# Projections and the last feed-forward piece by token half, and each feed-forward as one stage

## The chip, the cores and the metric

The kernel runs as one program on one core of a Trainium2 chip. The metric is the time of one execution in microseconds (us). The engines are TensorE (PE; its weight loads are shown as PEld), VectorE (DVE), ScalarE (ACT), GpSimd (POOL) and SyncE (SP), which here only issues DMAs. Each engine runs its own list of instructions in order, and semaphores order the engines among each other.

## The reference, cut to what matters

A residual `x` of 1024 tokens by 1024 features (and a context of 256 tokens) passes two mixing layers and then a second block. Every layer begins with a norm over the features of a token and ends with a projection whose result is added to `x`:

```python
x = x + gt * (y @ out_e)                    # even layer, with context; then norm_o, in_o
x = x + gt * (y @ out_o)                    # odd layer (RWKV scan and a convolution)
x = rmsnorm(x, final_g)
x = layernorm(ALPHA * x + 0.5 * swiglu(x, ffn1_w1, ffn1_w3, ffn1_w2), ln1_g, ln1_b)
m = mixer(x, w_in, ...) @ w_out             # sparse attention and a gated MLP
x = layernorm(ALPHA * x + m, ln2_g, ln2_b)
x = layernorm(ALPHA * x + 0.5 * swiglu(x, ffn2_w1, ffn2_w3, ffn2_w2), ln3_g, ln3_b)

def swiglu(x, w1, w3, w2): return (silu(x @ w1) * (x @ w3)) @ w2     # 1024 -> 2816 -> 1024
```

A norm needs sums over all 1024 features of a token, so it needs the whole result of the projection before it for that token, and nothing of other tokens.

## The kernel before, in words

**Layout.** `xT` stays on the chip: 128 partitions, `KD` = 8 feature tiles, 1280 columns of tokens (1024 and the context). Tokens are worked in chunks: `MAIN_CHUNKS` are two halves of 512, `ALL_CHUNKS` adds the 256 of the context.

**Products in two parts.** Each fp32 operand is cut in a high part (ScalarE, `high_part`) and the rest as low part (VectorE, `low_part`), both as fp32r. `Weights.product` issues for each of the k tiles of 128 features three matmuls: high by high, high by low, low by high (lines 318, 319, 320). An output tile of 128 features over 1024 tokens is 2 x 8 x 3 = 48 matmuls of 512 columns.

**The weight ring.** `Weights` has two slots of raw, high and low weights. `load` waits until the slot's raw weights have been cut and issues a DMA on SP's queue, `cut_high` waits for the DMA and for the tile that used the slot before, `cut_low` follows on VectorE. `in_turn` writes ScalarE's and VectorE's order: weights of tiles 0 and 1, then for each tile m first the cut for m + 2 and then the work that finishes tile m. The ring belongs to a stage (`nc.Block`): a stage's first load is issued when all engines have left the stage before.

**Heads.** A stage begins with a head that makes the parts of its right operand: `Cut` (and `LoadedCut`, from `y_out` in DRAM) or `Norm`. ScalarE and VectorE do the first two weight cuts and then the head. A `Norm` with `centre` subtracts the mean, squares on ScalarE into two buffers, and sums with matmuls by `avg` on the PE (line 420), for both halves; then for each chunk come the root, the reciprocal (line 465), the scaling (468) and the parts (450, 482). GpSimd adds the bias to `xT` later.

**Combine stages** (`out_e`, `out_o`, `out_2`). 8 tiles over all chunks. VectorE adds each tile to `xT` (`gated_update`, line 672; `deepnorm_update`, line 680). `Totals` adds up the tiles (squares of ScalarE where the next norm does not centre), and `Totals.reduce` makes the mean on the PE behind the last tile (lines 187, 191).

**Feed-forward** (`ffn_stage`). The hidden 22 tiles are worked in `PIECES` of 8, 8 and 6. Each piece is two stages: `up`, two tiles (w1, w3) for a hidden unit, gated and cut on ScalarE and VectorE, and `down`, `product_stage` with 8 output tiles. That is six stages, each with its own ring. `out_stage` does the last norm and stores the output.

Of the kernel before, what the change touches and what calls it, by code (L numbers as in the profile page):

```python
# [8 lines left out]
P = 128  # L9
# [73 lines left out]
def program(nc, A):  # L83
# [16 lines left out]
    with root:  # L100
# [55 lines left out]
        class Totals:  # L156


            def __init__(self, ctx, name, chunks, squares):
                self.chunks, self.squares = chunks, squares  # L160
                width = chunks[-1][0] + chunks[-1][1]
                space = sb(ctx, f"{name}_totals", [P, 3 if squares else 1, width])
                self.acc, self.sq, self.width = space[:, 0], space[:, 1:3] if squares else None, width

            def tile(self, n):
                return self.sq[:, n % 2] if self.squares else xT[:, n, 0:self.width]

            def square(self, act, n):

                if n >= 2:  # L170
                    act.wait_ge(summed.h, summed.base + n - 1)
                nc.scalar.activation(self.sq[:, n % 2], xT[:, n, 0:self.width], ACT.Square).then_inc(squared.h, 1)

            def add(self, dve, n):
                if self.squares:
                    dve.wait_ge(squared.h, squared.base + n + 1)
                if n == 0:
                    nc.vector.tensor_copy(self.acc, self.tile(0)).then_inc(summed.h, 1)
                else:
                    dve.wait_ge(summed.h, summed.base + n)  # L180
                    nc.vector.tensor_tensor(self.acc, self.acc, self.tile(n), ALU.add).then_inc(summed.h, 1)

            def reduce(self, pe):
                n = KD - 1
                pe.wait_ge(summed.h, summed.base + n)
                for c, (t, w) in enumerate(self.chunks):
                    nc.tensor.matmul(bank(STAT_BANKS[c], w), avg[:, :], self.acc[:, t:t + w], start=True, stop=False)
                if self.squares:
                    pe.wait_ge(squared.h, squared.base + KD)
                for c, (t, w) in enumerate(self.chunks):  # L190
                    nc.tensor.matmul(bank(STAT_BANKS[c], w), avg[:, :], self.tile(n)[:, t:t + w], start=False,
                                     stop=True).then_inc(totalled.h, 1)

            def end(self):
                summed.base += KD - 1
                totalled.base += len(self.chunks)
                if self.squares:
                    squared.base += KD

        with ExitStack() as ctx:  # L200
# [5 lines left out]
            totals = Totals(ctx, "x", ALL_CHUNKS, True)  # L206
# [2753 lines left out]
```

## Time and profile before

| | |
|---|---|
| time, median of 3 runs | 4350.43 us (4343.89 to 4352.59) |
| profiled execution | 4352.45 us, its span 4350.5 us |
| PE busy | 3604.8 us, 83% of the span |
| VectorE busy | 1917.5 us, 44% |
| ScalarE busy | 1092.0 us, 25% |
| GpSimd busy | 84.7 us, 2% |
| mean granted TensorE clock of the span | 0.924 |
| DMA | 280.08 MB, mean 64 GB/s |

The span runs from the first to the last instruction. A matmul's end is modelled, so that the busy times of matmuls that follow each other closely overlap; their cost is better read from the distance of their starts. The idle time in brackets is that of the engine just before the instruction, with what released it. A granted clock of 1.00 is TensorE's upper level (2.4 GHz), 0.50 its lower one (1.2 GHz).

### The profile page before, as it was taken

To read this page: it belongs to the slowest core of one execution; us is meant where nothing else is said; L and a number is where in the kernel's file an instruction comes from. 1 tells how busy PE (TensorE), PEld (TensorE's weight loads), DVE (VectorE), ACT (ScalarE), POOL (GpSimd) and SP (SyncE) were. 2 spreads that over 40 slices of the span, in tenths; PEclk is the share of its full clock that TensorE was granted. 3 is DMA by queue.
4 is the path that set the end of the run, shared out by engine and by line. 5 is a ranking of instruction groups with operands and counts; after the bars stand their busy time and mean duration, and the time that the engine had idled before them with its cause. 6 is when DMAs were issued, how large, how long until landed. Compare 5 with 4: busy or idle time off the path is not lost. (4 is left out here: it accounts for less than half of the span.)

```text
span 4350.5 us, 67259 instructions
## 1 busy us (share of the span) xinstructions
PE 3604.8 (83%) x30260; PEld 2892.8 (66%) x30260; DVE 1917.5 (44%) x2670; ACT 1092.0 (25%) x1640; POOL 84.7 (2%) x83
## 2 busy tenths in 40 slices
PE   1999879997667777548999989889778979899997
PEld 1887668874256676436877778657556758777775
DVE  6554355445465556464211212267783352121224
ACT  2110221023333343212111101145464131011112
POOL 0000000000000000000000000020000020000000
PEclk9999999998589999769999999989899989999998
DMA  4232201223722212321111011111000111111111
GB/s 162 90 116 91 103 31 62 84 83 132 251 61 66 71 48 61 137 98 39 49 39 46 33 58 39 43 42 35 6 1 1 39 42 36 41 57 44 44 44 53
DMA packets 141677, 280.08 MB, mean 64 GB/s; under 512 B 7976, under 2 KB 83112, under 8 KB 141136
## 3 DMA queue, kind: packets, MB, share of 16 engines
q1 hardware_dynamic: 120912, 223.14, 16.0%
q10 hardware_dynamic: 20480, 52.65, 3.2%
q8 instruction: 238, 3.90, 0.4%
q14 instruction: 47, 0.39, 0.0%
HBM read 224.09 MB, written 51.42 MB: 63 GB/s over the span
## 5 line engine op out<-in xcount | busy, mean ns | idle before, releaser
L318 PE MATMUL PS<-ffn_x_high,ffn_up_wh 128*128 128x512 f32 x1408 | 554.7, 394 | 59.2 <-DVE ffn_up_wl L286 29.9
L319 PE MATMUL PS<-ffn_x_low,ffn_up_wh 128*128 128x512 f32 x1408 | 553.1, 393 | 0.0
L320 PE MATMUL PS<-ffn_x_high,ffn_up_wl 128*128 128x512 f32 x1408 | 552.7, 393 | 0.0
L286 DVE TENSOR_TENSOR ffn_up_wl<-ffn_up_raw,ffn_up_wh 128x1024 fp32r<-128x1024 f32 x88 | 108.4, 1232 | 648.0 <-ACT ffn_up_wh L283 647.8
L318 PEld LDWEIGHTS PS<-ffn_x_high,ffn_up_wh 128*128 128x128 f32 x1408 | 267.9, 190 | 119.0 <-DVE ffn_up_wl L286 31.6
L318 PE MATMUL PS<-ffn_hid_high,ffn_down_wh 128*128 128x512 f32 x704 | 281.1, 399 | 59.5 <-DVE ffn_down_wl L286 59.5
L320 PEld LDWEIGHTS PS<-ffn_x_high,ffn_up_wl 128*128 128x128 f32 x1408 | 267.4, 190 | 56.5
L319 PEld LDWEIGHTS PS<-ffn_x_low,ffn_up_wh 128*128 128x128 f32 x1408 | 267.7, 190 | 55.8
L319 PE MATMUL PS<-ffn_hid_low,ffn_down_wh 128*128 128x512 f32 x704 | 279.5, 397 | 0.0
L320 PE MATMUL PS<-ffn_hid_high,ffn_down_wl 128*128 128x512 f32 x704 | 279.1, 396 | 0.0
L283 ACT ACTIVATE ffn_up_wh<-ffn_up_raw 128x1024 fp32r<-128x1024 f32 x88 | 93.2, 1060 | 734.2 <-PE PS L320 594.8
L318 PE MATMUL PS<-in_o_high,in_o_wh 128*128 128x512 f32 (+1 forms) x608 | 229.0, 377 | 21.2 <-DVE in_o_low L482 18.6
L318 PE MATMUL PS<-in_e_high,in_e_wh 128*128 128x512 f32 (+1 forms) x576 | 209.7, 364 | 24.5 <-DVE in_e_low L482 23.1
L319 PE MATMUL PS<-in_o_low,in_o_wh 128*128 128x512 f32 (+1 forms) x608 | 228.0, 375 | 0.0
L320 PE MATMUL PS<-in_o_high,in_o_wl 128*128 128x512 f32 (+1 forms) x608 | 227.7, 375 | 0.0
L319 PE MATMUL PS<-in_e_low,in_e_wh 128*128 128x512 f32 (+1 forms) x576 | 206.2, 358 | 0.0
L320 PE MATMUL PS<-in_e_high,in_e_wl 128*128 128x512 f32 (+1 forms) x576 | 205.7, 357 | 0.0
L286 DVE TENSOR_TENSOR ffn_down_wl<-ffn_down_raw,ffn_down_wh 128x1024 fp32r<-128x1024 f32 (+1 forms) x48 | 54.5, 1137 | 326.4 <-ACT ffn_down_wh L283 326.4
L318 PEld LDWEIGHTS PS<-ffn_hid_high,ffn_down_wh 128*128 128x128 f32 x704 | 135.9, 193 | 90.7 <-DVE ffn_down_wl L286 62.0
L320 PEld LDWEIGHTS PS<-ffn_hid_high,ffn_down_wl 128*128 128x128 f32 x704 | 135.5, 193 | 29.1
L319 PEld LDWEIGHTS PS<-ffn_hid_low,ffn_down_wh 128*128 128x128 f32 x704 | 135.9, 193 | 28.3
L318 PEld LDWEIGHTS PS<-in_o_high,in_o_wh 128*128 128x128 f32 x608 | 115.5, 190 | 43.6 <-issue 18.6
(418 smaller groups left out, 6544.8 us busy)
## 6 DMA issues: line engine op xcount, KB each, us to landing
ffn_up_raw<-in_ffn_up SPq DMA_DIRECT2D x88, 512.0 KB, 3.5
norm_e_t<-in_ada SPq DMA_DIRECT2D x32, 512.0 KB, 4.1
in_o_raw<-in_in_o SPq DMA_DIRECT2D x32, 512.0 KB, 3.6
ffn_down_raw<-in_ffn_down SPq DMA_DIRECT2D x32, 512.0 KB, 3.6
scan_tin<-scan_in SPq DMA_DIRECT2D x10, 1536.0 KB, 10.1
scan_in<-um ACTq DMA_DIRECT2D x20, 641.0 KB, 5.0
in_e_raw<-in_in_e SPq DMA_DIRECT2D x24, 512.0 KB, 3.6
scan_tin<-scan_in SPq DMA_DIRECT2D x10, 1024.0 KB, 13.2
```

What stands on the lines that cost most here:

```text
L283: return nc.scalar.activation(out, x, ACT.Copy)
L286: return nc.vector.tensor_tensor(out, x, high.bitcast(fp32), ALU.subtract)
L318: nc.tensor.matmul(out, wh, xh, start=k == 0, stop=False)
L319: nc.tensor.matmul(out, wh, xl, start=False, stop=False)
L320: last = nc.tensor.matmul(out, wl, xh, start=False, stop=k == kt - 1)
```

## The change

- `Totals` takes groups of chunks. The three combine stages run over items (group, tile): eight tiles for the first half of the tokens, then the same eight for the rest, so every weight tile is loaded and cut twice. Each group is reduced on its own, the first behind item 8.
- `Norm` gets `early` chunks. For these the centring (behind item 8), squares (9), variance sums (10), root and reciprocal (11) and for norms in place the scaling (12, 13) are done inside the stage before. The next stage's head does only the rest. What a head does ahead of the first weight cuts moves to `lead_act` and `lead_dve`: centring, squares and variance sums of the second half, or the roots.
- `ffn_stage` is one block with one ring for all 76 items: 16 up, 8 down, 16 up, 8 down, 12 up, and 16 down items by half. At each change from up to down, the products of two tile halves are issued for all hidden units but the last, and then those for the last. PSUM is used in four quarters. The last feed-forward also holds the last norm and the stores of the output; `out_stage` and `project_stage` are gone.

The core of the diff:

```diff
 class Norm(Cut):
+    def lead_act(self, act):
+        for c in self.late():
+            if self.centre:
+                self.squares(act, c)
+            else:
+                self.root(act, c)
+
+    def lead_dve(self, dve):
+        if self.centre:
+            for c in self.late():
+                self.centre_chunk(dve, c)
+        if not self.early:
+            self.invert(dve, 0)
+        if not self.early or not self.in_place:
+            self.scale(dve, 0, range(KD))
...
+    def early_pe(self, pe, i):
+        if self.centre and i == 10:
+            self.var_sums(pe, 0)
+
+    def early_act(self, act, i, total):
+        if self.centre:
+            if i == 9:
+                self.squares(act, 0)
+            if i == 11:
+                self.root(act, 0)
+        elif i == 9:
+            act.wait_ge(totalled.h, total + 1)
+            self.root(act, 0)
+
+    def early_dve(self, dve, i, total):
+        if self.centre and i == 8:
+            dve.wait_ge(totalled.h, total + 1)
+            self.centre_chunk(dve, 0)
+        if i == 11:
+            self.invert(dve, 0)
+        if self.in_place and i in (12, 13):
+            self.scale(dve, 0, range(4 * (i - 12), 4 * (i - 12) + 4))
...
+def combine_stage(name, w_dram, rhs, chunks, groups, update, squares, norm, cut=Cut):
+    items = [(gi, m) for gi in range(len(groups)) for m in range(KD)]
...
+            for i, (gi, m) in enumerate(items):
+                s = i % 2
+                pe.wait_ge(w_low[s].h, w_low[s].base + i // 2 + 1)
+                pe.wait_ge(evacuated[s].h, evacuated[s].base + i // 2)
+                for c in groups[gi]:
...
+                    last = ring.product(pe, PS[:, at:at + w], s, parts, 0, KD, t, w, ready if m == 0 else None)
+                last.then_inc(tile_done[s].h, 1)
+                if i == KD:
+                    reduce(0)
+                norm.early_pe(pe, i)
+            reduce(1)
...
-def ffn_stage(name, w_up, w_down, head_of):
+def ffn_stage(name, w_up, w_down, head, norm, is_last):
     PIECES = [(0, 8), (8, 8), (16, 6)]
+    tiles = []
+    for p, (first, n_hid) in enumerate(PIECES):
+        both = [("down", p, m, (0, 1)) for m in range(KD)]
+        if p == len(PIECES) - 1:
+            both = [("down", p, m, (c,)) for c in range(2) for m in range(KD)]
+        tiles += [("up", p, m, (0, 1)) for m in range(2 * n_hid)] + both
...
+                            if kind == "down" and m == 0 and chunks[0] == 0:
+                                first, n_hid = PIECES[p]
+                                pairs = (first + n_hid) // 2
+                                turns = [(g, 0), (g, 1)] if chunks == (0, 1) else [(g, 0), (g + 1, 0)]
+                                pe.wait_ge(stored[0].h, stored[0].base + pairs)
+                                pe.wait_ge(stored[1].h, stored[1].base + pairs - 1)
+                                for q, c in turns:
+                                    product(q, c, range(n_hid - 1))
+                                pe.wait_ge(stored[1].h, stored[1].base + pairs)
+                                for q, c in turns:
+                                    product(q, c, range(n_hid - 1, n_hid))
+                                g = turns[-1][0] + 1
+                                continue
+                            for c in chunks:
+                                product(g, c)
+                            if g == TAIL + KD:
+                                reduce(0)
+                            norm.early_pe(pe, g - TAIL)
...
-        with ExitStack() as odd:
-            combine_stage("out_o", A["out_o"], yT, MAIN_CHUNKS, gated_update(mods["o"][2], False), True)
+            with ExitStack() as odd:
+                combine_stage("out_o", A["out_o"], yT, MAIN_CHUNKS, BY_CHUNK, gated_update(mods["o"][2]), True, final_norm)
+            ffn_stage("ffn1", A["ffn1_up"], A["ffn1_down"], final_norm, ln1, False)
+                mixer_stage(mT, ln1)
+                combine_stage("out_2", A["w_out"], mT, MAIN_CHUNKS, BY_CHUNK, deepnorm_update, False, ln2)
+            ffn_stage("ffn2", A["ffn2_up"], A["ffn2_down"], ln2, ln3, True)
```

## Rows read from the trace of the kernel before

**Rows 1.** Groups by line: busy us, mean ns | idle before, releasers.
```profile
L318 PE MATMUL PS<-ffn_x_high,ffn_up_wh 128*128 128x512 f32 x1408 | 554.7, 394 | 59.2 <-DVE ffn_up_wl L286 29.9 <-DVE ffn_x_low L286 16.8 <-DVE ffn_x_low L482 12.5
...
L318 PE MATMUL PS<-ffn_hid_high,ffn_down_wh 128*128 128x512 f32 x704 | 281.1, 399 | 59.5 <-DVE ffn_down_wl L286 59.5
```

**Rows 2.** Timeline of PE, feed-forward 1: start, us, engine line op [idle before].
```profile
2223.29 0.79 PE L318 MATMUL PS<-ffn_hid_high,ffn_down_wh 128*128 128x512 f32 x1 [10.49 <-DVE ffn_down_wl L286]
...
2320.85 0.80 PE L318 MATMUL PS<-ffn_x_high,ffn_up_wh 128*128 128x512 f32 x1 [7.46 <-DVE ffn_up_wl L286]
...
2507.17 0.80 PE L318 MATMUL PS<-ffn_hid_high,ffn_down_wh 128*128 128x512 f32 x1 [10.15 <-DVE ffn_down_wl L286]
```

**Rows 3.** Timeline of ACT and DVE, one tile of the second combine stage.
```profile
1960.21 1.06 ACT L283 ACTIVATE out_o_wh<-out_o_raw 128x1024 fp32r<-128x1024 f32 x1 [6.27 <-PE PS L320]
...
1961.30 1.23 DVE L286 TENSOR_TENSOR out_o_wl<-out_o_raw,out_o_wh 128x1024 fp32r<-128x1024 f32 x1 [6.11 <-ACT out_o_wh L283]
...
1964.85 1.23 DVE L181 TENSOR_TENSOR out_o_totals<-out_o_totals 128x1024 f32<-128x1024 f32 x1 [1.13 <-ACT out_o_totals L172]
...
1971.09 1.06 ACT L283 ACTIVATE out_o_wh<-out_o_raw 128x1024 fp32r<-128x1024 f32 x1 [6.27 <-PE PS L320]
```

**Rows 4.** Timeline of DVE: the last update of four stages.
```profile
594.17 1.68 DVE L672 SCALAR_TENSOR_TENSOR xT<-PS,mod_eg,xT 128x1024 f32<-128x1024 f32 x2 [9.27 <-PE PS L320]
...
2014.55 1.28 DVE L672 SCALAR_TENSOR_TENSOR xT<-PS,mod_og,xT 128x1024 f32<-128x1024 f32 x1 [7.24 <-PE PS L320]
...
2814.18 1.22 DVE L680 SCALAR_TENSOR_TENSOR xT<-xT,PS 128x1024 f32<-128x1024 f32 x1 [5.68 <-PE PS L320]
...
3482.27 1.22 DVE L680 SCALAR_TENSOR_TENSOR xT<-xT,PS 128x1024 f32<-128x1024 f32 x1 [8.40 <-PE PS L320]
```

**Rows 5.** Timeline of PE: the first product of five stages.
```profile
96.04 0.77 PE L318 MATMUL PS<-in_e_high,in_e_wh 128*128 128x512 f32 x1 [21.86 <-DVE in_e_low L482]
...
617.37 0.76 PE L318 MATMUL PS<-in_o_high,in_o_wh 128*128 128x512 f32 x1 [17.76 <-DVE in_o_low L482]
...
2035.76 0.76 PE L318 MATMUL PS<-ffn_x_high,ffn_up_wh 128*128 128x512 f32 x1 [16.79 <-DVE ffn_x_low L286]
...
2857.59 0.76 PE L318 MATMUL PS<-in_high,in_wh 128*128 128x512 f32 x1 [9.41 <-DVE in_low L482]
...
3523.05 0.77 PE L318 MATMUL PS<-ffn_x_high,ffn_up_wh 128*128 128x512 f32 x1 [9.41 <-DVE ffn_x_low L482]
```

**Rows 6.** Timeline of the closing stage: PE, DVE and SP's queue.
```profile
4307.02 1.98 PE L187 MATMUL PS<-ffn_down_totals,avg 128*128 128x512 f32 x4 [1.31 <-DVE xT L680]
...
4313.41 15.70 PE L420 MATMUL PS<-xT,avg 128*128 128x512 f32 x32 [2.69 <-ACT xT L432]
...
4328.93 3.35 DVE L465 RECIPROCAL ln_std<-ln_std 128x512 f32<-128x512 f32 x1 [8.74 <-ACT ln_std L438]
...
4334.51 13.04 SPq L638 DMA_DIRECT2D out<-xT  x8
```

**Rows 7.** Windows: busy us and count of each engine, PEclk, DMA share, GB/s.
```profile
2215.00:2223.00 8.00, 0.00 (x0) 0.00 (x0) 2.22 (x2) 1.52 (x3) 0.00 (x0) 0.53 0.42 132
...
2223.00:2228.00 5.00, 4.71 (x11) 3.75 (x12) 1.46 (x2) 0.81 (x1) 0.00 (x0) 0.50 0.64 185
...
200.00:300.00 100.00, 96.80 (x502) 82.60 (x502) 56.40 (x72) 10.80 (x10) 0.00 (x0) 1.00 0.32 109
```

**Rows 8.** Timeline of ACT in the last down piece of feed-forward 1.
```profile
2773.44 0.84 ACT L283 ACTIVATE ffn_down_wh<-ffn_down_raw 128x768 fp32r<-128x768 f32 x1 [7.32 <-PE PS L320]
```

**Rows 9.** Timeline at two seams: SP's queue, ACT and DVE.
```profile
2019.24 76.66 SPq L299 DMA_DIRECT2D ffn_up_raw<-in_ffn_up  x9
...
2022.77 1.06 ACT L283 ACTIVATE ffn_up_wh<-ffn_up_raw 128x1024 fp32r<-128x1024 f32 x1 [5.84 <-DMA ffn_up_raw<-in_ffn_up]
...
2029.62 5.39 DVE L468 SCALAR_TENSOR_TENSOR xT<-xT,vec,final_norm_std 128x512 f32<-128x512 f32 x8
...
2829.32 9.13 DVE L458 TENSOR_TENSOR xT<-xT,PS 128x1024 f32<-128x1024 f32 x8
```

More of the change, by code:

```diff
@@ L156, in program @@
         class Totals:
[L159 to L174, printed above, removed]
+            def __init__(self, ctx, name, chunks, squares, groups):
+                self.chunks, self.squares, self.groups = chunks, squares, groups
+                width = max(self.span(gi)[1] for gi in range(len(groups)))
+                self.acc = sb(ctx, f"{name}_totals", [P, chunks[-1][0] + chunks[-1][1]])
+                self.sq = sb(ctx, f"{name}_squares", [P, 2, width]) if squares else None
@@ new lines, in span, with tile, square @@
+            def span(self, gi):
+                t = self.chunks[self.groups[gi][0]][0]
+                return t, sum(self.chunks[c][1] for c in self.groups[gi])
+            def tile(self, gi, n):
+                t, w = self.span(gi)
+                return self.sq[:, (gi * KD + n) % 2, 0:w] if self.squares else xT[:, n, t:t + w]
+            def square(self, act, gi, n):
+                t, w = self.span(gi)
+                i = gi * KD + n
+                if i >= 2:
+                    used, at = divmod(i - 2, KD)
+                    if at == KD - 1:
+                        act.wait_ge(totalled.h, totalled.base + sum(len(q) for q in self.groups[:used + 1]))
+                    else:
+                        act.wait_ge(summed.h, summed.base + used * (KD - 1) + at + 1)
+                nc.scalar.activation(self.tile(gi, n), xT[:, n, t:t + w], ACT.Square).then_inc(squared.h, 1)
@@ L393, in program, with __init__, at, counts @@
         class Norm(Cut):
-            def __init__(self, ctx, name, parts, chunks, eps, centre, gain, bias, in_place, var_banks=(2, 5)):
-                super().__init__(xT, parts, KD, chunks)
-                self.eps, self.centre, self.gain, self.bias, self.in_place = eps, centre, gain, bias, in_place
-                self.var_banks = var_banks
-                self.std = sb(ctx, f"{name}_std", [P, len(chunks), 512])
-                self.t_buf = None if in_place else sb(ctx, f"{name}_t", [P, 2, KD, 512])
+            def __init__(self, std, name, chunks, eps, centre, gain, bias, in_place, early):
+                super().__init__(xT, None, KD, chunks)
+                self.std = std
+                self.name, self.eps, self.centre, self.gain, self.bias, self.in_place = name, eps, centre, gain, bias, in_place
+                self.early, self.t_buf, self.ahead = early, None, {}
+            def at(self, q):
+                return q.base + self.ahead.get(q, 0)
+            def counts(self):
+                n = len(self.chunks)
+                per = {std_ready: n, rstd_ready: n, scaled: n * KD}
+                if self.centre:
+                    per.update({cen_ready: 4 * n, sq_ready: 4 * n, var_summed: 4 * n})
+                return per
+            def place(self, ctx, parts):
+                self.parts = parts
+                if not self.in_place:
+                    self.t_buf = sb(ctx, f"{self.name}_t", [P, 2, KD, 512])
+            def late(self):
+                return range(self.early, len(self.chunks))
             def t(self, c, k):
@@ new lines, in ffn_stage, with mixer_stage @@
+                for s in range(2):
+                    w_loaded[s].base += 16 * (n_tiles // 2)
+                    for q in (w_high, w_low, tile_done, evacuated):
+                        q[s].base += n_tiles // 2
+                    for q in (gated, stored):
+                        q[s].base += sum(n for _, n in PIECES) // 2
+                head.end()
+                norm.ahead = {}
+                high_ready.base += sum(n for _, n in PIECES)
+                totals.end()
+        def mixer_stage(mT, head):
```

645 lines of the change are left out of this document (320 added, 325 removed).

## The prediction

> **What bounds the kernel now.** I read the profile in this order: the groups of instructions by line, TensorE's waits in order of time, the same stretches on the other engines, and last the granted clock. The groups show two heavy families, the up products (1408 triples of matmuls) and the down products (704) of the two feed-forwards [rows 1]. Their idle time names the weight cut on VectorE that ends it: 29.9 us and 59.5 us. The timeline places those waits. None lies inside a stage. Each stands where one stage ends and the next begins: up to down the PE waits 10.49, then 10.15 us, down to up 7.46 us [rows 2]. Each feed-forward has five such places. The ten waits add up to 89.4 us, exactly the sum of the two idle times in [rows 1]. Inside a stage the PE is the bound: two cuts of ScalarE are 10.88 us apart for a tile of 48 matmuls, so one matmul of 512 columns costs 0.2267 us, and ScalarE is idle 6.27 us before its cut [rows 3]. So the kernel is bound by the PE within stages and by a serial chain (DMA, ScalarE's cut, VectorE's cut) at every seam. The other seams are those with a norm. The last product of a stage ends where VectorE's last update starts: 594.17, 2014.55, 2814.18 and 3482.27 us [rows 4]. The next stage's first product starts at 617.37, 2035.76, 2857.59 and 3523.05 [rows 5]. The seams are thus 23.2, 21.2, 43.4 and 40.8 us long, and from the last product (1.31 us ahead of 4307.02, [rows 6]) to the end of the span at 4350.5 it is 44.8 us. The clock adds to each: in the wait the granted clock was 0.53, and in the 5 us after it 0.50, the lower level of 1.2 GHz [rows 7].
>
> **One ring and one stage for the feed-forward.** What goes: ten waits, 89.4 us. The next weights are loaded and cut while the two tiles before run. A slot is cut again when its own tile is done, and there is still a whole tile (10.88 us) for a cut of 1.06 and one of 1.23 [rows 3]. What could take their place is the last hidden unit. After the last up tile it needs a cut on each engine (1.06, 1.23), then the product (about 1.22, as an update of that width in [rows 4]), its high part (1.06) and its low part (1.23), some 6.0 us with hand-overs. The change issues all but the last unit's products for two halves first: 2 x 7 x 3 x 0.2267 = 9.5 us, in the last piece 2 x 5 x 3 x 0.2267 = 6.8 us. Both cover 6.0, so I cost this at nothing. If that cover failed altogether, it would be 6 us at six places.
>
> The slow restart goes too. The first down piece ran from 2223.29 to 2313.39 (2320.85 less 7.46), 90.1 us, where 8 x 10.88 = 87.04 and 0.16 for the modelled end are due: 2.9 us lost. The second up piece ran from 2320.85 to 2497.02 (2507.17 less 10.15), 176.2 us instead of 174.2: 1.9 us lost [rows 2]. At the mean of these two, 2.4 us, ten restarts are 24 us. Sum: 89.4 + 24.0 = **113.4 us**.
>
> **Products by half.** The number of matmuls is the same, only weights are loaded and cut twice in the three projections and the two last pieces. A half item is 24 x 0.2267 = 5.44 us, in the last down piece 4.08 (a tile there is 7.32 + 0.84 = 8.16 us, [rows 8]). Per half item ScalarE and VectorE work in a chain: cut 1.06, cut 1.23, update 1.28/2, square 1.06/2, add 1.23/2, some 4.1 us [rows 3, 4]. That is under 5.44, so nothing is lost. In the last down piece there is no square and the cut is 0.84 [rows 8], so it is about 3.1 under 4.08. A weight load lands 3.5 us after its issue (2019.24 to 2022.77, [rows 9]), and its slot is free for two half items, 8 to 11 us. The 24 extra loads of the projections and 16 of the last pieces stand on SP's queue with nothing else behind them that is due; the output's stores for the second half come after the last load has landed. Queued behind the early norm on VectorE are the cuts of items 11 to 15. The centring is 4 x 1.14 = 4.6 us, the reciprocal 3.35, two scalings of four are 2.7 each [rows 6, 9]. Against items of 4.08 us VectorE is about 1 us late at the last item of each feed-forward, and on time against 5.44. ScalarE stands in its third square until the PE has begun the variance sums; behind it is the cut of item 12, which the PE wants only after item 11, 4.08 us later. On the PE's own queue the first half's sums move in front of products that were never late. Its two reducing matmuls are four records in about 1.9 us [rows 6], and for a layer norm eight variance matmuls, sixteen records, about 6.9 us at full clock (0.43 us a record). These are counted as costs below.
>
> **Seam by seam** (old length, less new length, less what moved onto the PE; the new length counts only the chain that ends last).
> - *Start of the first projection.* The root, reciprocal (3.35) and first scaling (5.39) now run in the time in which the weights load, and before they came behind the weight cuts. What no longer stands in the chain is the load (3.5) and ScalarE's cut (1.06) [rows 9]; some 0.6 comes back, since VectorE's second cut no longer runs beside the root. The wait of 21.86 us ahead of 96.04 [rows 5] loses **4.0**.
> - *First combine to the odd projection.* Update 1.1, square 0.8, reducing about 1.5, stage change 0.3, then VectorE's scaling of 5.4, two cuts of 2.5 and the first low part 0.7, and hand-overs: 12.6. 23.2 - 12.6 - 1.9 = **8.7**.
> - *Second combine to feed-forward 1.* The first half is scaled already, so the weights end last: update and square 1.3, reducing 0.9, stage change 0.3, load 3.5, cuts 1.06 + 2.46, first parts 0.7: 10.2. 21.2 - 10.2 - 1.9 = **9.1**.
> - *Feed-forward 1 to the mixer.* VectorE 1.7 late with its update, reducing 1.9, stage change and small memsets 1.0, centring and squaring the second half's first pair 2.3. Then comes the ring of squares and sums, whose fourth square ends 6.6 after that. Only behind it stand the weight cuts 1.06 + 1.06 + 1.23 and the first low part 0.7, with hand-overs 17.9. 43.4 - 17.9 - 1.9 - 6.9 = **16.7**.
> - *Third combine to feed-forward 2.* The same chain with the update on time (1.0 less) and no memsets (0.7 less): 16.2. 40.8 - 16.2 - 8.8 = **15.8**.
> - *The end.* Update 1.7, reducing 1.9, first square after 2.3, variance sums 8.9, root 0.7, reciprocal 3.35, scaling 5.39, bias 0.7, store and end 3.3: 28.3. The 8.9 is half of a stretch of 15.7 us for 32 records [rows 6] and one microsecond for its slow start. 44.8 - 28.3 - 8.8 = **7.7**.
>
> Together 62.0. What the second halves need afterwards (reciprocal, scaling, low parts before the PE has run two half tiles of the first half) stands at the same distance from the first product as before, so small waits there stay. The bias on GpSimd is untouched.
>
> **Sum.** 113.4 + 62.0 = 175.4 us. The profiled execution took 4352.45 us with a span of 4350.5, 2.0 us above the median of 4350.43. From the median: 4350.4 - 175.4, about **4175 us**.
>
> **Bounds of the unknown.** No row shows half items. If each of the 16 in a feed-forward's last piece were held to the projections' 5.5 us instead of 4.08, that is 2 x 16 x 1.4 = 45 us. From below, a chain may cost nothing, and the clock may no longer fall in the shortened seams, which gives 2.4 at each of two, and variance sums at full clock 2 each at three: 11 us more gain, and about 9 us for my hand-overs. I take nothing for the unknown since the chain in [rows 3] leaves room. Both ends stay in the range.
>
> **Rivals.**
> - *Half items are too short (12%).* VectorE's queue becomes the bound in the last pieces because norm, cut, update and add share it. For: 4.08 us are few, and the early norm takes 13 us of VectorE in eight items. Against: the rows sum to less. It gives 10 to 45 us, most likely near 4205.
> - *The up-to-down wait stays (5%).* The last hidden unit, not the weights, then ends last. For: VectorE and ScalarE do a cut for the next slot ahead of it. Against: 6.0 under 6.8 us. Six waits of 6 us and restarts of 2.4: 50 us, 4225.
> - *The clock falls in half items, slower (2%).* Every half item now has its own wait on the PE's queue. If each drops the clock to 1.2 GHz, the 48 half items of the projections and 32 of the last pieces run at half speed. That adds 2 x 16 x 5.44 + 110 + 32 x 4.08 = 415 us, so 4590. It turns the sign once more than 42% of those matmuls are slow. Against: from 200 to 300 us the PE was busy 96.80 of 100 us with waits in between, at a clock of 1.00 [rows 7].
> - *The change doesn't do what it says (2%).* The early norm waits until the stage's end, and the ring for its stage. Then it is within 10 us of before.
>
> The Trainium skill has the third as a failure that was seen: in "TensorE: Matmul & The Clock Gate", section "A second HAM failure mode: psum-queue depth-cycling", short idles between groups of matmuls that cycle through banks make the clock fall and rise again. By that rule the sum would be the 4590 above, by the row it is 4175. The case's trace so far has no such swing inside a stage.
>
> **How the numbers follow.** Likeliest case 79%, at 4175, with its own range of 4155 to 4195. To hold eight in ten with the first rival's nearer part, the range is 4152 to 4212. A measurement of this kernel tells a difference of about 0.2% (9 us) from none. Faster 0.96 (the likeliest, the first two rivals), same 0.02 (the change does nothing), slower 0.02 (the clock).
>
> **What would show it.** In the profile after: no wait of the PE over 1 us inside either feed-forward, and a tile every 10.88 us across what were stage boundaries. A clock of 1.00 there. The first product after the combines and feed-forward 1 comes 12.6, 10.2, 17.9 and 16.2 us after the last one. Cuts in the last down piece stand 4.08 us apart, except around the variance sums (7 us). Wrong would be: waits of the PE on the weight cut of items 11 to 15, on the low part of the last hidden unit, or 512-column matmuls 0.43 us apart within a stage.

## The result, and the profile after

The changed kernel takes **4181.9 us** (median of four runs, 4180.1 to 4183.2) beside 4349.7 us for the kernel before, a ratio of 0.9616 with a 95% interval of 0.9599 to 0.9632. Run once more later, it came out the same by ratio (4185.9 us, 0.9616, 0.9600 to 0.9631). The forecast was 4175 us with a range of 4152 to 4212. The profiled execution took 4181.0 us, with a span of 4179.2 where it was 4350.5: 171.3 us less.

The groups of instructions by line show the product lines of the feed-forwards. The numbers behind the second bar are the idle time of TensorE (PE) just before them: first all of it, then what ended most of it.

```profile
L334 PE MATMUL PS<-ffn_x_high,ffn_wh 128*128 128x512 f32 x1408 | 549.8, 390 | 15.7 <-DVE ffn_x_low L302 9.4
...
L334 PE MATMUL PS<-ffn_hid_high,ffn_wh 128*128 128x512 f32 x704 | 276.0, 392 | 2.6 <-DVE ffn_wl L302 2.6
```

Beside [rows 1], the 59.5 us ahead of down products have become 2.6, and the 29.9 us that a weight cut put ahead of up products are gone. What stays ahead of them are the seams. The windows say the same for a stretch of 600 us inside feed-forward 1, first the kernel before (busy us and count of PE, its weight loads, VectorE, ScalarE and GpSimd, then the granted clock, DMA share and GB/s):

```profile
2100.00:2700.00 600.00, 564.57 (x2448) 465.38 (x2447) 123.57 (x103) 88.84 (x86) 0.00 (x0) 0.97 0.14 45
```

and the changed kernel:

```profile
2100.00:2700.00 600.00, 598.69 (x2641) 495.42 (x2640) 140.62 (x126) 98.11 (x97) 0.00 (x0) 1.00 0.16 50
```

PE is busy for 598.69 of 600 us, and the 1.31 us missing are one wait. It is the only one over 1 us between its first and its last product. The timeline of PE has it, with the first products that answer to [rows 5] and the last product of each feed-forward:

```profile
92.75 0.76 PE L334 MATMUL PS<-in_e_high,in_e_wh 128*128 128x512 f32 x1 [18.66 <-DVE in_e_low L547]
...
606.64 0.77 PE L334 MATMUL PS<-in_o_high,in_o_wh 128*128 128x512 f32 x1 [8.79 <-DVE in_o_low L547]
...
2013.04 0.76 PE L334 MATMUL PS<-ffn_x_high,ffn_wh 128*128 128x512 f32 x1 [8.87 <-DVE ffn_x_low L302]
...
2678.12 0.50 PE L334 MATMUL PS<-ffn_hid_high,ffn_wh 128*128 128x512 f32 x1 [1.31 <-DVE ffn_wl L302]
...
2744.08 0.39 PE L336 MATMUL PS<-ffn_hid_high,ffn_wl 128*128 128x512 f32 x1
...
2761.68 0.47 PE L334 MATMUL PS<-in_high,in_wh 128*128 128x512 f32 x1 [1.87 <-DVE in_low L547]
...
3416.51 0.47 PE L334 MATMUL PS<-ffn_x_high,ffn_wh 128*128 128x512 f32 x1 [1.87 <-DVE ffn_x_low L547]
...
4152.22 0.39 PE L336 MATMUL PS<-ffn_hid_high,ffn_wl 128*128 128x512 f32 x1
```

The last updates of the three projections start at these times, where VectorE is on time and so marks the end of the last product, as in [rows 4]:

```profile
594.22 1.14 DVE L682 SCALAR_TENSOR_TENSOR xT<-PS,mod_eg,xT 128x512 f32<-128x512 f32 x2 [5.33 <-PE PS L336]
...
2001.58 0.75 DVE L682 SCALAR_TENSOR_TENSOR xT<-PS,mod_og,xT 128x512 f32<-128x512 f32 x1 [0.40 <-PE PS L336]
...
3400.40 0.69 DVE L688 SCALAR_TENSOR_TENSOR xT<-xT,PS 128x512 f32<-128x512 f32 x1 [3.20 <-PE PS L336]
```

So the seams are 12.4 us (606.64 - 594.22), 11.5, 17.2 (2761.68 - 2744.47) and 16.1 us long, and from the last product to the end of the span it is 26.6 us (4179.2 - 4152.61). They were 23.2, 21.2, 43.4, 40.8 and 44.8.

In the last down piece ScalarE's weight cuts show the pace of the half items:

```profile
2690.76 0.84 ACT L299 ACTIVATE ffn_wh<-ffn_raw 128x768 fp32r<-128x768 f32 x1 [3.23 <-PE PS L336]
2694.84 0.84 ACT L299 ACTIVATE ffn_wh<-ffn_raw 128x768 fp32r<-128x768 f32 x1 [3.23 <-PE PS L336]
...
2732.04 0.84 ACT L299 ACTIVATE ffn_wh<-ffn_raw 128x768 fp32r<-128x768 f32 x1 [1.23 <-PE PS L336]
2736.12 0.85 ACT L299 ACTIVATE ffn_wh<-ffn_raw 128x768 fp32r<-128x768 f32 x1 [3.23 <-PE PS L336]
```

These pairs stand 4.08 us apart, and ScalarE is idle for 1.23 to 3.23 us before each cut. PE is never made to wait there for the early norm, whose variance sums are in its own queue:

```profile
2716.73 7.03 PE L458 MATMUL PS<-xT,avg 128*128 128x512 f32 x16
```

### The profile page after: what moved, and what is told of

It reads as the page before. It is cut to its first block and busy times, and to the rows that moved or that the text cites. A ratio compares the mean times of both kernels' runs of the same rounds, so it can differ in the third digit from the quotient of the medians.

```text
span 4179.2 us, 67465 instructions
## 1 busy us (share of the span) xinstructions
PE 3579.7 (86%) x30260; PEld 2877.8 (69%) x30260; DVE 1967.4 (47%) x2785; ACT 1130.0 (27%) x1696; POOL 80.0 (2%) x83
## 5 line engine op out<-in xcount | busy, mean ns | idle before, releaser
L302 DVE TENSOR_TENSOR ffn_wl<-ffn_raw,ffn_wh 128x1024 fp32r<-128x1024 f32 (+1 forms) x152 | 177.5, 1168 | 1017.5 <-ACT ffn_wh L299 1017.5
L334 PE MATMUL PS<-ffn_x_high,ffn_wh 128*128 128x512 f32 x1408 | 549.8, 390 | 15.7 <-DVE ffn_x_low L302 9.4
L335 PE MATMUL PS<-ffn_x_low,ffn_wh 128*128 128x512 f32 x1408 | 549.1, 390 | 0.0
L336 PE MATMUL PS<-ffn_x_high,ffn_wl 128*128 128x512 f32 x1408 | 549.1, 390 | 0.0
L334 PEld LDWEIGHTS PS<-ffn_x_high,ffn_wh 128*128 128x128 f32 x1408 | 265.2, 188 | 74.6 <-issue 12.3
L336 PEld LDWEIGHTS PS<-ffn_x_high,ffn_wl 128*128 128x128 f32 x1408 | 265.0, 188 | 55.2
L335 PEld LDWEIGHTS PS<-ffn_x_low,ffn_wh 128*128 128x128 f32 x1408 | 265.1, 188 | 54.8
L334 PE MATMUL PS<-ffn_hid_high,ffn_wh 128*128 128x512 f32 x704 | 276.0, 392 | 2.6 <-DVE ffn_wl L302 2.6
L336 PE MATMUL PS<-ffn_hid_high,ffn_wl 128*128 128x512 f32 x704 | 273.9, 389 | 0.0
L335 PE MATMUL PS<-ffn_hid_low,ffn_wh 128*128 128x512 f32 x704 | 273.9, 389 | 0.0
L334 PE MATMUL PS<-in_o_high,in_o_wh 128*128 128x512 f32 (+1 forms) x608 | 229.2, 377 | 12.4 <-DVE in_o_low L547 9.7
L334 PE MATMUL PS<-in_e_high,in_e_wh 128*128 128x512 f32 (+1 forms) x576 | 211.3, 367 | 20.1 <-DVE in_e_low L547 18.7
## 6 DMA issues: line engine op xcount, KB each, us to landing
scan_tin<-scan_in SPq DMA_DIRECT2D x10, 1536.0 KB, 10.1
```

The lines of the kernel that those rows point to most:

```text
L302: return nc.vector.tensor_tensor(out, x, high.bitcast(fp32), ALU.subtract)
L334: nc.tensor.matmul(out, wh, xh, start=k == 0, stop=False)
L335: nc.tensor.matmul(out, wh, xl, start=False, stop=False)
L336: last = nc.tensor.matmul(out, wl, xh, start=False, stop=k == kt - 1)
```

## The experiments

All ratios are to the kernel before on the same chip. At 4350 us a difference of 0.001 is 4.35 us. The intervals of a ratio are some 0.0015 to each side, about 7 us, and a difference of two ratios is good to about 10 us. So a term of a few microseconds is read from the traces and not from the times.

### Is the stage end worth 113 us, and is the clock a part of its price?

**One.** The changed kernel, with the ten stage ends put back as waits: before each change of kind SP loads nothing ahead, and the cuts of the two next tiles come after the last work of the old kind.

```
+ if g in WALLS and kind == "down":
+     sp.wait_ge(stored[1].h, stored[1].base + (first + n_hid) // 2)
+ elif g in WALLS:
+     i, b, s = turn(g - 1)
+     sp.wait_ge(evacuated[b].h, evacuated[b].base + 2 * i + 2)
- steps = in_turn(n_tiles, cut, finish)
+ steps = in_turn_walls(n_tiles, cut, finish, WALLS)   # ScalarE and VectorE
```

> The changed kernel with the waits of the ten stage ends inside the two feed-forwards put back: at each change between up and down the next two weight loads are issued only when the work of the piece before is finished, and their cuts come behind it. All else as changed. If the waits and the restarts at the lower clock are what the single stage saves (theory), this is 113 us slower than the changed kernel's 4181.9, so 4295, with waits of the PE of about 10 us (up to down) and 7.5 us (down to up). Rival: the load and cut of the next weights were not what ended last, and the gain came from the ring's continuity in another way; then it is within 30 us of 4182.

Measured: 4295.7 us, ratio 0.9866 (0.9851 to 0.9881), which is 109 us above the changed kernel (0.9866 - 0.9616 = 0.0250). The first two of the ten waits in PE's timeline:

```profile
2204.61 0.77 PE L334 MATMUL PS<-ffn_hid_high,ffn_wh 128*128 128x512 f32 x1 [10.06 <-DVE ffn_wl L302]
...
2301.26 0.79 PE L334 MATMUL PS<-ffn_x_high,ffn_wh 128*128 128x512 f32 x1 [7.34 <-DVE ffn_wl L302]
```

All ten add up to 87.7 us, so by the ratios some 21 us lie outside the waits. The trace says it more finely. From first to last product the two feed-forwards take 786.7 and 793.0 us where the changed kernel takes 731.4 and 736.1, together 112.1 us more. Of these, 24.4 lie outside the waits.

**Two.** The same, and PE runs dummy matmuls during the waits, whose results are overwritten.

```
+ if g in WALLS:
+     i, b, s = turn(g)
+     pe.wait_ge(evacuated[b].h, evacuated[b].base + 2 * i)
+     for _ in range(40 if kind == "down" else 28):
+         nc.tensor.matmul(PS[:, quarter(g):quarter(g) + 512], x.high[:, 0, 0:P],
+                          x.high[:, 0, 0:512], start=True, stop=True)
```

> As the kernel with the ten waits put back, but the PE runs 40 (up to down) or 28 (down to up) matmuls of 512 columns during each wait, whose results are overwritten; they are work that the reference does not need. They fill 9.1 and 6.3 us, less than the waits. If the restart at the lower clock is a cost of its own of 2.4 us each (theory), the time is 24 us under the kernel with idle waits: 4271, and the granted clock in the feed-forwards is 1.00. Rival: the 24 us were not the clock but other small waits at a stage's start; then it equals the kernel with idle waits, 4295.

Measured: 4273.0 us, ratio 0.9810 (0.9794 to 0.9827), 22.6 us below the first. In the traces the two feed-forwards are together 21.2 us shorter (777.0 and 781.5 us), 2.1 us for each of ten restarts. The windows show where. First the kernel with idle waits, in a wait and in the 5 us behind it:

```profile
2195.00:2204.00 9.00, 0.00 (x0) 0.00 (x0) 3.03 (x3) 2.86 (x3) 0.00 (x0) 0.70 0.35 117
2204.00:2209.00 5.00, 4.39 (x11) 3.55 (x12) 1.54 (x2) 0.31 (x1) 0.00 (x0) 0.51 0.64 197
```

then the one with dummy matmuls:

```profile
2203.00:2212.00 9.00, 9.00 (x41) 7.32 (x39) 2.45 (x2) 2.12 (x2) 0.00 (x0) 1.00 0.34 117
2213.00:2218.00 5.00, 4.49 (x20) 3.76 (x21) 1.48 (x2) 0.24 (x1) 0.00 (x0) 1.00 0.65 187
```

In 5 us behind the wait PE ran 11 matmuls at a granted clock of 0.51 (1.2 GHz) in the one, and 20 at 1.00 (2.4 GHz) in the other. So a wait costs more than its length, and 21.2 of the 24.4 us beyond the waits go when PE is kept busy: that part is the clock.

### Does the last hidden unit need its cover?

**Three.** PE waits for all hidden units, and not for all but the last, before the first products of each down piece.

```
- pe.wait_ge(stored[1].h, stored[1].base + pairs - 1)
+ pe.wait_ge(stored[1].h, stored[1].base + pairs)
```

> The changed kernel, only that the PE waits for the last hidden unit's low part before it issues any down product, instead of doing the other units' products first. Theory: the unit is ready 6.0 us after the last up tile (cut, cut, product, high part, low part), so six waits of the PE of 6 us each appear and, where the clock falls for it, up to 2.4 us more each: 4218 to 4232. Rival: the unit is ready earlier or the wait is covered otherwise, then 4182.

Measured: 4230.4 us, ratio 0.9715 (0.9701 to 0.9730), 43 us above the changed kernel. The six waits are 5.99, 5.99, 5.51, 5.99, 5.99 and 5.51 us, together 35.0. The profile calls the releaser "issue", but the rows of VectorE in that wait show what is awaited, its cut, the gate product and the low part:

```profile
2191.56 1.22 DVE L302 TENSOR_TENSOR ffn_wl<-ffn_raw,ffn_wh 128x1024 fp32r<-128x1024 f32 x1 [9.65 <-ACT ffn_wh L299]
2192.70 1.21 DVE L2247 SCALAR_TENSOR_TENSOR xT<-xT,PS 128x1024 f32<-128x1024 f32 x1
2195.04 1.23 DVE L302 TENSOR_TENSOR ffn_hid_low<-xT,ffn_hid_high 128x1024 fp32r<-128x1024 f32 x1 [1.12 <-ACT ffn_hid_high L299]
```

The low part ends at 2196.27 and PE starts at 2196.36. The forecast's 6.0 us for this chain is right, and the other units' products do cover it: the changed kernel shows no such wait. In the trace the two feed-forwards are 47.4 us longer than in the changed kernel (754.9 and 760.0 us), so 12.4 lie beyond the waits, 2.1 for each of six restarts. The window behind the first wait has a granted clock of 0.65:

```profile
2196.00:2201.00 5.00, 4.63 (x14) 3.76 (x15) 0.26 (x1) 0.00 (x0) 0.00 (x0) 0.65 0.00 0
```

### Where do the seams' 58 us come from?

**Four.** The halves stay, but nothing of the norm is done early.

```
- if self.centre and i == 10:                  # early_pe
+ if self.early and self.centre and i == 10:
...
+ if not self.early:                           # early_act and early_dve
+     return
...
- norm_o = Norm(..., False, 1)                 # and the four other norms
+ norm_o = Norm(..., False, 0)
```

So the first half's squares, variance sums, root, centring, reciprocal and scaling stand in the head of the next stage (for the last norm at the end of its own), ahead of those of the second half.

> The edit: output projections and the last feed-forward piece still run by token half, the feed-forwards are still one stage, but nothing of the first half's norm is done during the second half: its variance sums, centring, reciprocal, squares and root are back in the head of the next stage (and at the end). Theory of the prediction: the one ring is worth 113, the seams 62, and almost all of the 62 comes from the norm done early, since halves alone only shorten nothing: the closings of the seams go back to their former lengths (17.7, 16.8, 43.4, 40.8 less at most 3 each, the end about 44), and the time rises by 50 to 62 us over the changed kernel, to 4230 to 4245, ratio 0.972 to 0.976. Rival 'the order by halves itself gives the gain' (the first half's reduction and update are done before the second half ends, so the closing is half as long anyway): a rise of only 20 to 35 us, ratio 0.966 to 0.970.

Measured: 4217.8 us, ratio 0.9691 (0.9673 to 0.9708), 33 us above the changed kernel by the ratios and 32 by the medians on one chip. This expectation of mine was wrong. The result lies in its rival's range, though the next experiment shows that the rival's reason, the halves themselves, is not the right one either. The seams were 17.8, 15.5, 35.1 and 34.7 us and the end 40.5: each is shorter than before by four to eight microseconds, though all the norm is back in them. PE's timeline ahead of the mixer shows one reason:

```profile
2756.06 15.47 PE L458 MATMUL PS<-xT,avg 128*128 128x512 f32 x32 [3.32 <-ACT xT L469]
...
2785.04 0.77 PE L334 MATMUL PS<-in_high,in_wh 128*128 128x512 f32 x1 [13.51 <-DVE in_low L547]
```

The variance sums wait 3.32 us and not 12.5 (2831.68 after 2819.16 before). Before, VectorE made the two weight cuts ahead of the centring, and they waited for a load; in [rows 9] the centring starts only at 2829.32. The change had put the norm's first steps ahead of the cuts in every head. So the next two experiments test the order in the head.

**Five.** Kernel four with the cuts ahead again, at ten places of ScalarE and VectorE:

```
- head.lead_act(act)
  next(steps)
+ head.lead_act(act)
```

> The kernel with the halves kept and nothing of the norm early (ratio 0.9691 when run), and one edit more: at every head the cuts of the first two weight tiles come before the norm's first steps on ScalarE and VectorE, as they did in the kernel before. The question is what the 'halves alone' gain of that kernel was. In it, the wait between the closing's reduction and the first squares was 3.32 and 2.69 us at the two layer-norm seams, against 12.52 and 9.76 before, because the centring no longer stands behind weight cuts that wait for a load; its price was the cuts (2.0 on ScalarE, 2.35 on VectorE) behind the squares. Theory 'it was the order in the head, not the halves': 9.2 - 4.3 = 4.9 and 7.1 - 4.3 = 2.8 come back at these two seams, about 4.1 at the start of the first projection, 3.5 before the odd projection and 3.8 before feed-forward 1, together 19: a ratio of 0.9735. The halves alone are then worth about 5 us. Rival 'it was the halves': the seams stay within 5 us in all, 0.969 to 0.9702.

Measured: 4239.7 us, ratio 0.9751 (0.9735 to 0.9767), 26 us above kernel four. The forecast was 19 us, a ratio of 0.9735. The wait is back:

```profile
2770.82 15.60 PE L458 MATMUL PS<-xT,avg 128*128 128x512 f32 x32 [12.47 <-ACT xT L469]
...
2795.77 0.76 PE L334 MATMUL PS<-in_high,in_wh 128*128 128x512 f32 x1 [9.34 <-DVE in_low L547]
```

and in VectorE's rows the centring stands behind the cuts:

```profile
2766.15 2.40 DVE L302 TENSOR_TENSOR in_wl<-in_raw,in_wh 128x1024 fp32r<-128x1024 f32 x2 [6.88 <-ACT in_wh L299]
2768.47 9.13 DVE L485 TENSOR_TENSOR xT<-xT,PS 128x1024 f32<-128x1024 f32 x8
```

The seams are 21.4, 19.6, 40.2 and 37.7 us and the end 40.5, together 15.9 us longer than in kernel four, and the first product comes 3.4 us later (95.87 for 92.48). So the traces place 19 us of the difference, and the ratios leave it between 16 and 36. Against the 23.2, 21.2, 43.4, 40.8 and 44.8 of the kernel before, the seams are 14.0 us shorter. The first half's reduction, 1.9 us, was moved into each of the five stages before them, which takes 9.5 of them back. The halves alone are worth about 4.5 us.

**Six.** The same edit on the changed kernel itself.

> The changed kernel with the same edit alone: at every head the cuts of the first two weight tiles come before the norm's first steps, everything early stays early. Theory: the second half's centring and squares wait for the load again (9.2 and 7.1 us later), less the cuts that no longer stand behind them (3.4): 5.9 at the seam into the mixer and 3.7 ahead of feed-forward 2; the first scaling waits for load and cut at the start of the first projection (3.3) and before the odd projection (4.1); before feed-forward 1 the weights end last anyway, 0. Together 17: a ratio of 0.9655 where the changed kernel has 0.9616. Rival 'with the first half's norm done early the order in the head has cover': under 5 us, 0.9616 to 0.9628.

Measured: 4204.1 us, ratio 0.9664 (0.9646 to 0.9682), 21 us above the changed kernel. The seam into the mixer is 24.8 us (17.2), the one before feed-forward 2 20.7 (16.1), the one before the odd projection 17.2 (12.4), the first wait of PE 21.7 (18.7), and the one before feed-forward 1 is unchanged at 11.6. That is 7.6, 4.6, 4.8 and 3.0, together 20. In all four places something of the norm waits for a load that it does not need.

### What sets the small waits that stayed?

**Seven.** ScalarE's order at the layer-norm seams: two squares, the weight cuts, two squares, four high parts, and then the second half's root.

```
- self.squares(act, c)            # in lead_act
+ self.squares(act, c, range(2))
+ self.squares(act, 1, range(2, 4))   # in on_act, ahead of the high parts
+ if self.centre and c == 0 and k == 4:
+     self.root(act, 1)
```

> The changed kernel with ScalarE's order at the head of the mixer and of feed-forward 2 altered: two of the four squares, then both weight cuts, then the two other squares, and the second half's root after four of the first half's high parts. In the changed kernel the weight cuts stand behind all four squares (PE waits 1.87 us ahead of the first product) and the reciprocal waits behind the low parts and root (4.26 us ahead of the second half). Theory: ScalarE's order sets both waits; the first goes to about 0 and the second to 2 to 3 us, 3 to 4 us less at each of two seams: 4175. Rival: VectorE's queue alone (centring, cuts, low parts, reciprocal, scaling) sets them, then the sum of the two waits stays at 6.1 us a seam and the time at 4182.

Measured: 4179.9 us, ratio 0.9602 (0.9587 to 0.9617): not told apart from the changed kernel by time. In the trace PE's wait of 1.87 us before the first product is gone (at one of the seams 1.18 us stand inside the variance sums in its place), while the wait for the second token half stayed at 3.91 and 4.23 us. Half of the theory holds.

**Eight.** GpSimd adds the bias to the stored sum only when all low parts are made.

```
+ pool.wait_ge(parts_ready.h, parts_ready.base + self.count(len(self.chunks) - 1, KD - 1))
  for c, (t, w) in enumerate(self.chunks):
```

> The edit: at every seam with a bias held back (ffn1 to mixer, out_2 to ffn2, and the start of nothing else), GpSimd adds the bias to the stored sum only when all sixteen low parts of the stage ahead are made, where it now follows each low part. At these two seams of the changed kernel the wait for the second token half is 4.26 us, against 3.20 and 3.11 in the kernel before, and eight low parts of the first half take 6.61 us in place of 5.38. Theory 'VectorE and GpSimd slow each other': with GpSimd idle in that stretch a low part goes back from 0.82 to 0.67 us, the second-half wait falls from 4.26 to about 2.9 at both seams, and the time falls by 2 to 3 us, to a ratio of 0.9610 (after: 0.9616). Rival 'no contention, the wait is set by ScalarE's high parts or by order': low parts and wait stay within 0.2 us and so does the time. Second rival: the bias that comes later holds up the next work that reads the sum; then a wait for GpSimd of over 1 us shows inside the next stage and the ratio rises.

Measured: 4180.7 us, ratio 0.9603 (0.9587 to 0.9619), not told apart by time (the unchanged kernel beside it had 0.9616). The trace decides. First the changed kernel in the seam to the mixer, VectorE and GpSimd:

```profile
2760.79 6.61 DVE L547 SCALAR_TENSOR_TENSOR in_low<-xT,vec,in_high 128x512 fp32r<-128x512 f32 x8
2767.32 3.34 DVE L491 RECIPROCAL norm_std<-norm_std 128x512 f32<-128x512 f32 x1
2770.70 6.69 DVE L499 SCALAR_TENSOR_TENSOR xT<-xT,vec,norm_std 128x512 f32<-128x512 f32 x8
...
2761.63 14.78 POOL L581 TENSOR_SCALAR xT<-xT,vec 128x512 f32<-128x512 f32 x8 [1076.61 <-DVE in_low L547]
```

then this kernel:

```profile
2771.19 3.35 DVE L491 RECIPROCAL norm_std<-norm_std 128x512 f32<-128x512 f32 x1
2774.57 5.39 DVE L499 SCALAR_TENSOR_TENSOR xT<-xT,vec,norm_std 128x512 f32<-128x512 f32 x8
...
2785.36 25.65 POOL L582 TENSOR_SCALAR xT<-xT,vec 128x512 f32<-128x512 f32 x16 [1096.04 <-DVE in_low L547]
```

Eight scalings take 6.69 us beside GpSimd's additions and 5.39 without them. The second-half wait is 2.72 and 2.73 us, where the changed kernel beside it had 3.69 and 4.23. With GpSimd out of the stretch VectorE's eight scalings are 1.3 us shorter and its eight low parts 1.2 us (5.38 for 6.61), and the two waits fall by 2.5 us in all. The difference of the times has the same sign and lies within its interval.

**Nine: a faster version.** Seven and eight together, and one raw weight buffer for all stages, so that the first two weight tiles of each later stage are loaded at the end of the stage before.

```
+ def load_ahead(sp, n, srcs):
+     for s, src in enumerate(srcs):
+         sp.wait_ge(w_low[s].h, w_low[s].base + n)
+         sp.dma_start(w_raw[:, s], src).then_inc(w_loaded[s].h, 16)
+ load_ahead(sp, n_items // 2, following)    # last on SP's list of a stage
```

> The changed kernel with three edits more: the raw weight buffer of two tiles is one for all stages and the first two weight tiles of each later stage are loaded at the end of the stage before it, so that their 3.1 us landing is over when the stage begins; ScalarE's order at the seams (two squares, then cuts, then the rest), and GpSimd's bias after all low parts. Theory: the first waits at the starts of out_e, out_o, out_2 and the seam after out_o, which end in a weight load or its cut, lose about 3 us each, and the order and the bias give 2 to 6, so 4162 to 4172 where the changed kernel takes 4182, ratio 0.957 to 0.959. Rival: at every one of these starts the weights are hidden behind the norm's or the transposed tiles' chain, so that only the second part counts: 0.960 to 0.9615.

Measured: 4155.1 us, ratio 0.9546 (0.9531 to 0.9562), 31 us below the changed kernel on the same chip, more than the theory had. Its rival is out. The waits at the starts of the three projections' stages and the seam after the second:

```profile
1901.71 0.76 PE L335 MATMUL PS<-out_o_high,out_o_wh 128*128 128x512 f32 x1 [19.55 <-DVE out_o_low L303]
...
1999.93 0.77 PE L335 MATMUL PS<-ffn_x_high,ffn_wh 128*128 128x512 f32 x1 [5.08 <-DVE ffn_x_low L303]
...
3280.97 0.77 PE L335 MATMUL PS<-out_high,out_wh 128*128 128x512 f32 x1 [5.17 <-DVE out_low L303]
```

The unchanged kernel beside it had 23.19, 8.82 and 9.36 there, and 19.13 for 16.69 ahead of the first combine: 14 us. The seams into the mixer and feed-forward 2 are 14.8 and 12.6 us long (18.7 and 16.1), with second-half waits of 2.63 and 2.61 (3.69 and 4.23): 10 us. That makes 24. Some 2 us more are the clock: behind the wait of 2.61 us in feed-forward 2 it did not fall, while behind the unchanged kernel's 4.23 us it did. The windows of the two, this kernel first:

```profile
3404.80:3409.80 5.00, 4.93 (x21) 4.01 (x22) 4.65 (x8) 0.11 (x1) 0.25 (x1) 1.00 0.00 0
```

```profile
3442.50:3447.50 5.00, 4.96 (x15) 3.94 (x16) 5.00 (x7) 0.08 (x1) 4.92 (x3) 0.66 0.00 0
```

The 5 us that are left I did not place, and they are within the interval.

**The changed kernel once more**, on the chip of four, eight and nine.

> The changed kernel itself once more, unedited, to be compared with the three above on one chip: a ratio of 0.9616 within 0.0016, gaps of PE as in its first trace (1.51, 3.32, 1.87 and 4.26 at the seam into the mixer).

Measured: 4185.9 us, ratio 0.9616 (0.9600 to 0.9631), with waits of 1.48, 3.31, 1.87 and 3.69 us at the seam into the mixer. The last had been 4.26, so that wait varies by 0.6 us from run to run.

## Why the prediction was right

The size was right within 7 us, and nearly every term stands in the trace close to its forecast size. That the sum of the seams is right within 1 us is partly luck, since misses of either sign cancel in it. The small errors lie at these steps.

- **One ring and one stage: 113.4 forecast.** First product to last product end went from 778.4 to 731.4 us in feed-forward 1 and from 782.7 to 736.1 in feed-forward 2, though 1.9 + 6.9 = 8.8 us of matmuls moved into each. That is 47.0 + 46.6 + 17.6 = **111.2 us**. Undoing it costs 109 by the ratios and 112.1 by the traces. Its parts hold too: 89.4 of waits (87.7 put back), and a restart at 2.4 us (2.1 by the dummy matmuls). The 2.4 came from two rows of 2.9 and 1.9. Over the first 120 matmuls behind each of the ten waits, the trace of the kernel before shows losses of 1.6 to 3.0 us with a mean of 2.4, so that two rows gave the mean was luck. The price of 6 us for a lost cover of the last hidden unit was 5.5 to 6.0 when it was taken away.
- **Half items cost nothing.** The chain of cuts and update kept under 4.08 us, and the early norm found room beside it. One wait came that the sum did not have, 1.31 us at the third item of each last down piece. The order of the last hidden unit makes it: the first two half items both keep that unit's products for the end, so both end close together and neither slot is free before. ScalarE's and VectorE's rows show the two cuts that the third and fourth items wait for:

```profile
2676.23 1.58 ACT L299 ACTIVATE ffn_wh<-ffn_raw 128x768 fp32r<-128x768 f32 x2 [3.42 <-PE PS L336]
```

```profile
2677.11 0.96 DVE L302 TENSOR_TENSOR ffn_wl<-ffn_raw,ffn_wh 128x768 fp32r<-128x768 f32 x1 [3.04 <-ACT ffn_wh L299]
```

PE goes on at 2678.12. The cover that I costed at nothing thus costs 1.3 us twice. VectorE was late at the last item as forecast: its last update starts at 2745.25, 0.8 us after the last product.
- **The seams: 62.0 forecast.** New lengths were 12.6, 10.2, 17.9, 16.2 and 28.3 by forecast and 12.4, 11.5, 17.2, 16.1 and 26.6 in the trace. With what moved taken as forecast (1.9 at two, 8.8 at three), the five terms are 8.9, 7.8, 17.4, 15.9 and 9.4 for 8.7, 9.1, 16.7, 15.8 and 7.7. The variance sums that moved took 7.03 us (6.9). The start of the first projection gave 3.3 for 4.0 (92.75 for 96.04). Together 62.7. The largest misses: before feed-forward 1 the load's second tile came 1.9 us after the first, and the chain was 1.3 longer; at the end the variance sums took 7.13 and not 8.9.
- **The rest.** 111.2 + 62.7 = 173.9, and the span fell by 171.3. The 2.6 us are differences of both signs elsewhere, nearly all in stages that the change does not touch: the first projection gave back 2.7 us, from there through the second combine 5.4 were gained, and from the mixer through the third combine 5.2 were lost, 4.4 of them in mixer and attention, at a granted clock of 0.91 where it was 0.93. I made no experiment on them. They are of the size by which runs of one kernel differ: between the odd projection and the second combine the changed kernel took 899.4 us in one profile and 907.1 in the other.
- **The rivals.** The clock did not fall in half items: the window of the second combine's half items has 364 matmuls in 83 us, 0.228 us apart, at a granted clock of 1.00.

```profile
1915.00:1998.00 83.00, 83.00 (x364) 67.99 (x364) 46.63 (x57) 26.33 (x33) 0.00 (x0) 1.00 0.24 77
```

But the prediction misread one thing here. It said that the trace of the kernel before has no swing of the clock inside a stage. It has, in the scan of the odd layer: between 1380 and 1740 us the clock fell ten times, though PE never waited more than 2.1 us. The timeline of PE in the kernel before, and the window around it:

```profile
1486.37 0.69 PE L1619 MATMUL PS<-XT,TT 64*64 64x64 f32 x32 [1.90 <-DVE TT L1432]
1488.98 1.13 PE L1619 MATMUL PS<-XT,TT 64*64 64x64 f32 x32 [1.92 <-DVE TT L1432]
```

```profile
1488.00:1492.00 4.00, 3.02 (x90) 3.06 (x92) 0.83 (x2) 1.20 (x2) 0.00 (x0) 0.57 0.01 4
```

The rule of the Trainium skill ("TensorE: Matmul & The Clock Gate", section "A second HAM failure mode: psum-queue depth-cycling") speaks of short idles between groups of matmuls of 512 columns that make the clock fall and rise. The scan's matmuls have 64, but its rows agree: waits of 1.90 and 1.92 us, and a granted clock of 0.57. The half items had none, since PE was busy for 83.00 of 83.00 us: each semaphore was up before PE asked for it. So the rival failed for want of idle time, and what idles between half items would have cost is not shown.

The wait from up to down products did not stay.

What the prediction did not see is the composition of its 62. It summed each seam's new chain rightly, with the weight cuts behind the squares, but did not say that the order in the head was worth more than the halves. Undoing one thing after another gives, by the ratios and so to some 10 us each, 26 us for the order in the head and 33 for the norm done early, and the 108 that are left (1 - 0.9751) are the ring, the stage and the halves together. The traces are finer: 111 for the ring and the stage, 4.5 for the halves, 19 for the order in the head, and 38 for the early norm (the seams of kernel four are together 59.5 us longer than the changed kernel's, and 21 us of variance sums moved). The last three are the 62, within 1 us. The halves by themselves are worth next to nothing. They are what makes the early norm possible.

## What to carry to other kernels

A stage end costs the length of its load-and-cut chain plus the slow restart (here 7.3 to 10.5 us and 2.4 us more), so where two stages can share one weight ring, let them be one. At the head of a stage, put on each queue what is ready first; an instruction that waits for a load should not stand ahead of one that doesn't (about 20 us here, for swapping two lines at ten places). Splitting the last work by halves pays little in itself, and mostly through what the first half lets start; and the first weights of the next stage can be loaded before this one ends if they have a buffer that outlives it (about 3.5 us a seam).

## What the hardware showed that I had not expected

- The price of a slow restart varied more from place to place than with the length of the wait. In the 5 us behind a wait of 10.1 us PE ran 11 matmuls at a granted clock of 0.51, behind one of 6.0 us 14 at 0.65, and 20 at 1.00 where it had been kept busy with dummy matmuls. But behind a wait of 10.18 us in the kernel before it ran 14 at 0.66 as well:

```profile
3714.00:3719.00 5.00, 4.80 (x14) 3.82 (x15) 1.37 (x2) 0.11 (x1) 0.00 (x0) 0.66 0.65 202
```

The levels are 1.2 and 2.4 GHz, and a mean between them is a window in which it changed.
- VectorE is slower beside GpSimd's additions to `xT`: 0.84 us for a 128x512 scaling where it is 0.67 alone, and 0.83 for a low part where it is 0.67. The bias "in the background" of the change's seams lay on the chain of the second half.
- The reciprocal was not slowed (3.34 us beside GpSimd, 3.35 alone).
